# Conditioning columns turned by VectorE in PSUM, router weights asked for later, GpSimd's product in three parts, and early loads for the second and fourth expert

## What is computed

```
mod = silu(c) @ w_ada + b_ada            # 6 x 1024 columns
shift_m, scale_m, gate_m, shift_f, scale_f, gate_f = split(mod, 6)
h = rms_norm(x, g_mix) * (1 + scale_m) + shift_m
x = x + gate_m * hybrid_mixer(h)         # h @ w_in; sparse + forgetting attention; @ w_out
h = rms_norm(x, g_ffn) * (1 + scale_f) + shift_f
x = x + gate_f * hierarchical_moe(h)     # 4 groups x 8 experts, 2 experts for a token
```

## Time and profile before

| | |
|---|---|
| timed, median of 3 runs | 787.77 us (786.98 to 788.53) |
| profiled execution, its own time | 783.2 us |
| its span (first to last instruction) | 781.3 us |
| TensorE busy | 746.2 us, 96% of the span, 3945 matmul records |
| VectorE busy | 351.7 us, 45% |
| ScalarE busy | 190.3 us, 24% |
| GpSimd busy | 56.2 us, 7% |
| DMA, over the whole span | 197.25 MB, mean 252 GB/s |

### The profile page before, as it was taken

How to read it: one execution, slowest core, us unless ns; L and a number is a source line. 1 busy time by engine, 2 the same in 40 slices (tenths; PEclk the granted TensorE clock), 3 DMA queues, 4 the chain that set the end, 5 groups by cost and what they waited for, 6 DMA issues and landing times.

```text
span 781.3 us, 9778 instructions
## 1 busy us (share of the span) xinstructions
PE 746.2 (96%) x3945; PEld 493.8 (63%) x3945; DVE 351.7 (45%) x751; ACT 190.3 (24%) x419; POOL 56.2 (7%) x56
## 2 busy tenths in 40 slices
PE   5999999999899999999979999999999999999996
PEld 3687778877433334343434688688888888885442
DVE  2026475664631212121211595455166565657445
ACT  5113332452411101110111408313141111111002
POOL 2213644000000000000001000000000000000000
PEclk9899999999999999999999999999999999999999
DMA  9896994644949999999999990233254636352401
GB/s 346 273 362 243 352 353 172 254 162 171 416 169 419 412 418 415 416 417 415 417 413 385 370 352 13 99 108 108 89 190 153 192 131 215 120 205 107 162 27 57
DMA packets 76632, 197.25 MB, mean 252 GB/s; under 512 B 3263, under 2 KB 37416, under 8 KB 70184
## 3 DMA queue, kind: packets, MB, share of 16 engines
q1 hardware_dynamic: 75632, 195.37, 66.4%
q0 software_dynamic: 288, 0.41, 0.4%
q10 hardware_dynamic: 664, 0.80, 0.4%
HBM read 195.33 MB, written 1.05 MB: 251 GB/s over the span
## 4 chain that ended last, share of the span: by engine, by line
PE 81%; SPq 8%; DMA 4%; DVE 4%; ACT 2%; issue 1%; DVEq 0%; ACTq 0%
PE ps L1495 17%; PE ps L1215 10%; PE ps L759 9%; PE ps L1556 8%; PE ps L901 8%; PE ps L1289 5%; SPq L575 4%; PE ps L1129 4%; DMA arena<-in_w_up 2%; SPq L581 2%; DMA ring<-in_w_in 2%; PE ps L779 2%; PE ps L912 2%; PE ps L1298 2%; PE ps L1091 2%; PE ps L1101 2%
## 5 line engine op out<-in xcount | busy, mean ns | idle before, releaser
L1215 PE MATMUL ps<-ring,arena 128*64 128x512 f32 x352 | 77.6, 593 | 2.1 <-DMA ring<-in_w_up 2.1
L901 PE MATMUL ps<-hs,ring 128*128 128x256 f32 (+1 forms) x288 | 69.5, 397 | 2.9 <-DMA ring<-in_w_in 2.9
L901 PEld LDWEIGHTS ps<-hs,ring 128*128 128x128 f32 (+1 forms) x288 | 54.0, 192 | 15.7 <-issue 9.4
L1215 PEld LDWEIGHTS ps<-ring,arena 128*64 128x64 f32 x352 | 25.9, 137 | 52.2 <-issue 52.2
L2826 DVE SCALAR_TENSOR_TENSOR arena<-arena,own_rows,ps 128x256 f32<-128x256 f32 x16 | 7.7, 481 | 111.2 <-ACT arena L1889 111.2
L759 PE MATMUL ps<-hs,ring 128*128 128x256 f32 x240 | 53.3, 381 | 0.3 <-PE ps L759 0.3
L759 PEld LDWEIGHTS ps<-hs,ring 128*128 128x128 f32 x240 | 45.2, 190 | 7.1 <-issue 0.9
L1495 PE MATMUL ps<-ring,hs 128*128 128x256 f32 x176 | 41.7, 380 | 0.9 <-DVE xT L2701 0.9
L1495 PE MATMUL ps<-ring,mixT 128*128 128x256 f32 x176 | 41.7, 380 | 0.0
L1495 PE MATMUL ps<-arena,mixT 128*128 128x256 f32 x176 | 41.6, 379 | 0.0
L1289 PE MATMUL ps<-ring,arena 128*64 128x512 f32 x176 | 40.2, 598 | 1.0 <-issue 0.5
(11 more groups left out here) (492 smaller groups left out, 1236.3 us busy)
## 6 DMA issues: line engine op xcount, KB each, us to landing
ring<-in_w_down SPq DMA_DIRECT2D x23, 1024.0 KB, 19.3
ring<-in_w_gate_up SPq DMA_DIRECT2D x22, 1024.0 KB, 7.4
ring<-in_w_gate SPq DMA_DIRECT2D x20, 1024.0 KB, 16.6
ring<-in_w_up SPq DMA_DIRECT2D x20, 1024.0 KB, 17.6
ring<-in_w_ada SPq DMA_DIRECT2D x5, 3072.0 KB, 14.3
ring<-in_w_down SPq DMA_DIRECT2D x5, 2048.0 KB, 7.9
ring<-in_w_in SPq DMA_DIRECT2D x9, 1024.0 KB, 18.5
ring<-in_w_ada SPq DMA_DIRECT2D x16, 512.0 KB, 11.0
```

What stands on the lines that cost most here:

```text
L901: last = pe.matmul(o[0:n, 0:L], lhsT=w[:, k, lo:lo + n], rhs=h[:, k, :], start=k == 0, stop=k == KT - 1)
L1215: last = pe.matmul(ps[WIN * h:WIN * (h + 1), 0, :].rearrange("p (g n) -> p g n", g=2), lhsT=xw[:, u, k, :], rhs=expert_gate_up(2 * n + h, ...
```

## The change

Five things change.

1. **Turning.** `quarters` now reads its moving operand as blocks of 32 columns with 96 left out between them, so that each group of 32 partitions holds the features of the quarters of every tile that belong to it. A 32x32 transpose on VectorE then turns rows into columns: for `scale_m` and `shift_m` from PSUM into SBUF (`row0`, 128x256), for the chunks in place in PSUM bank 7 (128x192). `ada_select`, `ada_cols` and ScalarE's copies are gone. What `ada_cols` did for the router behind chunks 3 and 4 stays, as `shift_f_products`.
2. **The start.** In the place of `ada_select(0)` stand four products 128x512 whose result nobody reads, as soon as the tokens are turned. The first load of chunk 0 is split in two (200 columns, then 128), and the order of the three features follows.
3. **Router weights.** The five loads and the memset ahead of them move behind GpSimd's work on chunk 0. Its work on each chunk becomes three products of 128x768 by a column and two sums, in the place of one product of 128x2304 and two sums.
4. **Early loads.** SP loads parts of experts 1 and 3 (the second and the fourth) earlier, two of them behind the last loads of the attention and two while the output products run.
5. **Experts.** `clear_banks` is no longer called: the first product into each bank half starts the sum instead. In odd teams one of the eight tiles of `combine_joined` moves ahead of the activation's turn.

The diff, cut to its core (`step`, `Q` = 32, `P` = 128, `L` = 256, `KT` = 8):

```diff
             load_ada0("scale", ADA_HALF)
-            sp.dma_start(w[:, :, 0:328], in_d[:, :, IQ + 256:BQ]).then_inc(in0_first, 16)
+            sp.dma_start(w[:, :, P:328], in_d[:, :, IQ + 384:BQ]).then_inc(in0_first, 16)
+            sp.dma_start(w[:, :, 0:P], in_d[:, :, IQ + 256:IQ + 384]).then_inc(in0_second, 16)
             load_ada0("shift", 0)
...
+            load_down(1)
+            load_down(3)
             sp.wait_ge(ada_rows_done, 9)
             load_gate_up(0)
...
+            sp.wait_ge(ob_done, 2)
+            load_half(1, 1)
+            sp.wait_ge(ob_done, 4)
+            load_half(3, 1)
             sp.wait_ge(mo_done, 4)
-            load_gate_up(1)
-            load_down(1)
+            load_half(1, 0)
...
             sp.wait_ge(mo_done, KT)
-            load_gate_up(3)
-            load_down(3)
+            load_half(3, 0)
...
-            pool.wait_ge(tile_ready, 1)
-            pool.memset(wr[:, :, GROUPS:GROUP_COLS], 0.0).then_inc(pad_ready, 1)
-            pool.dma_start(wr[:, :, 0:GROUPS], w_group[0].rearrange("(k p) g -> p k g", p=P)).then_inc(wr_there, 16)
...
-                pool.tensor_tensor(w[:, PE_K:KT, :], w[:, PE_K:KT, :],
-                                   silu_c[:, PE_K:KT].unsqueeze(2).broadcast_to([P, n, ada_width(c_)]), ALU.mult
-                                   ).then_inc(pool_step, 1)
+                pool.tensor_scalar(w[:, PE_K, :], w[:, PE_K, :], silu_c[:, PE_K:PE_K + 1], None, ALU.mult).then_inc(pool_step, 1)
+                pool.wait_ge(pool_step, step.up())
+                pool.tensor_scalar(w[:, PE_K + 1, :], w[:, PE_K + 1, :], silu_c[:, PE_K + 1:PE_K + 2], None, ALU.mult).then_inc(pool_step, 1)
                 pool.wait_ge(pool_step, step.up())
                 pool.tensor_tensor(w[:, PE_K, :], w[:, PE_K, :], w[:, PE_K + 1, :], ALU.add).then_inc(pool_step, 1)
-                pool.wait_ge(pool_step, step.up())
+                pool.tensor_scalar(w[:, PE_K + 2, :], w[:, PE_K + 2, :], silu_c[:, PE_K + 2:PE_K + 3], None, ALU.mult).then_inc(pool_step, 1)
+                pool.wait_ge(pool_step, step.up(2))
                 pool.tensor_tensor(w[:, PE_K, :], w[:, PE_K, :], w[:, PE_K + 2, :], ALU.add).then_inc(ada_pool_ready, 1)
+                if c_ != 0:
+                    continue
+                pool.memset(wr[:, :, GROUPS:GROUP_COLS], 0.0).then_inc(pad_ready, 1)
+                pool.dma_start(wr[:, :, 0:GROUPS], w_group[0].rearrange("(k p) g -> p k g", p=P)).then_inc(wr_there, 16)
...
             def quarters(bank, lhsT, rhs, first=False, last=False):
 
+                parts = rhs.rearrange("p (m g i) -> p m g i", g=4, i=Q)
                 n = rhs.shape[1] // 4
                 for g in range(4):
-                    mm = pe.matmul(ps[Q * g:Q * g + Q, bank, 0:n], lhsT=lhsT, rhs=rhs[:, n * g:n * g + n], start=first,
-                                   stop=last, skip_group_check=True)
+                    mm = pe.matmul(ps[Q * g:Q * g + Q, bank, 0:n].rearrange("p (m i) -> p m i", i=Q), lhsT=lhsT,
+                                   rhs=parts[:, :, g, :], start=first, stop=last, skip_group_check=True)
...
-            def ada_select(bank):
-
-                pe.wait_ge(row_taken, bank + 1)
-                for i in range(2):
-                    last = pe.matmul(ps[:, bank, i:KT:2], lhsT=row0[:, bank, i * P:(i + 1) * P], rhs=all_rows,
-                                     start=True, stop=True)
...
-            ada_select(0)
+            pe.wait_ge(xT_ready, 2)
+            for _ in range(4):
+                pe.matmul(ps[:, 3, :], lhsT=ones[:], rhs=xn[:, 1, 512:D], start=True, stop=True)
...
             features(0, 256, 72, h=h0, first=True)
+            features(0, P, h=h0)
+            pe.wait_ge(in0_second, 16)
             features(0, 0, h=h0)
-            features(0, P, h=h0)
             shift_tiles()
             chunk_there("in", 0)
-            features(0, chunk_q, h=h0, amid=lambda: ada_select(1))
+            features(0, chunk_q, h=h0)
...
             ada_rows(1)
             features(2, P)
-            ada_cols(1)
             turn_probs(0)
...
             ada_rows(3)
             features(3, P)
-            ada_cols(3)
+            shift_f_products(3)
             turn_probs(2)
...
                     last = pe.matmul(ps[:, 4 + t // 2, (t % 2) * L:(t % 2 + 1) * L], lhsT=y[:, (t % 4) * P:(t % 4 + 1) * P],
-                                     rhs=p, start=False, stop=False, skip_group_check=True)
+                                     rhs=p, start=m == 0 and t % 2 == 0, stop=False, skip_group_check=True)
...
                 if u:
                     turn_puts(m)
+                    if n > 1:
+                        combine_joined(m - 1, JOINED[5:6])
...
                 if n > 1:
-                    combine_joined(m - 1, JOINED[5:8] if u else JOINED[3:5])
+                    combine_joined(m - 1, JOINED[6:8] if u else JOINED[3:5])
...
                 gate_up(0, 0, first=True).then_inc(gu_done, 1)
-                clear_banks()
                 pe.wait_ge(act_ready, 2)
...
-            def take_row(c):
-                act.wait_ge(ada_rows_done, c + 4)
-                act.activation(row[:, 0:ada_width(c) // 4], ps[:, 7, 0:ada_width(c) // 4], ACT.Copy).then_inc(row_taken, 1)
...
-            ve.wait_ge(ada_done, 1)
-            ve.tensor_tensor(mod[:, 8:16], ps[:, 0, 0:KT], parA[:, b_lo + 8:b_lo + 16], ALU.add).then_inc(dve_step, 1)
+            ve.wait_ge(ada_rows_done, 1)
+            ve.transpose(row0, ps[:, 0, 0:KT * Q]).then_inc(dve_step, 1)
+            own()
+            ve.tensor_tensor(mod[:, 8:16], row0[:, 0:KT * Q:Q], parA[:, b_lo + 8:b_lo + 16], ALU.add).then_inc(dve_step, 1)
...
             def add_bias(c):
 
-                at, m = ada_columns(c)
-                ve.wait_ge(ada_done, c + 4)
+                n, m = ada_width(c) // 4, ADA_AT[c] // P
+                m = slice(m, m + n // Q)
+                ve.wait_ge(ada_rows_done, c + 4)
+                ve.transpose(ps[:, 7, 0:n], ps[:, 7, 0:n]).then_inc(row_taken, 1)
+                ve.wait_ge(row_taken, c + 3)
...
```

More of the change, by code:

```diff
@@ L293, in build @@
         xn = mixT[:].rearrange("p k t -> p (k t)").rearrange("p (b d) -> p b d", b=BLK)
-        row0 = cut(5888, 2, 256)
+        row0 = cut(5888, KT * Q)
         h0 = hs[:, 1]
@@ L298, in build @@
         fix = cut(6480, 5)
-        row = tokf[:, 1536:1728]
-        even_rows, odd_rows, all_rows = ident[:, 0:P:2 * Q], ident[:, Q:P:2 * Q], ident[:, 0:P:Q]
+        all_rows = ident[:, 0:P:Q]
         out_tmp = cut(8192, 2, 2, L)
@@ L733, in _ @@
+                pool.wait_ge(pool_step, step.up(2))
                 pool.tensor_tensor(w[:, PE_K, :], w[:, PE_K, :], w[:, PE_K + 2, :], ALU.add).then_inc(ada_pool_ready, 1)
+                if c_ != 0:
+                    continue
+                pool.memset(wr[:, :, GROUPS:GROUP_COLS], 0.0).then_inc(pad_ready, 1)
+                pool.dma_start(wr[:, :, 0:GROUPS], w_group[0].rearrange("(k p) g -> p k g", p=P)).then_inc(wr_there, 16)
+                for g in range(GROUPS):
+                    pool.dma_start(wr[:, :, GROUP_COLS + PER_GROUP * g:GROUP_COLS + PER_GROUP * (g + 1)],
+                                   w_router[0, g].rearrange("(k p) e -> p k e", p=P)).then_inc(wr_there, 16)
@@ L858, in ada_rows, with shift_f_products @@
                 quarters(7, ones[:, 0:Q], w[:, PE_K, :], last=True).then_inc(ada_rows_done, 1)
-            def ada_cols(c):
-                at = ada_columns(c)[0]
-                pe.wait_ge(row_taken, c + 5)
-                if ada_width(c) == 6 * P:
-                    pe.matmul(ps[:, 7, at.start:at.stop:3], lhsT=row[:, 0:P], rhs=even_rows, start=True, stop=True)
-                    pe.matmul(ps[0:64, 7, at.start + 1:at.stop:3], lhsT=row[:, P:192], rhs=even_rows, start=True, stop=True)
-                    pe.matmul(ps[64:P, 7, at.start + 1:at.stop:3], lhsT=row[:, 0:64], rhs=odd_rows, start=True, stop=True)
-                    last = pe.matmul(ps[:, 7, at.start + 2:at.stop:3], lhsT=row[:, 64:192], rhs=odd_rows, start=True,
-                                     stop=True)
-                else:
-                    pe.matmul(ps[0:64, 7, at], lhsT=row[:, 0:64], rhs=even_rows, start=True, stop=True)
-                    last = pe.matmul(ps[64:P, 7, at], lhsT=row[:, 0:64], rhs=odd_rows, start=True, stop=True)
+            def shift_f_products(c):
+                pe.wait_ge(row_taken, c + 3)
                 if c == 3:
@@ L961, in _ @@
             tokens(1, 0, 260, (1,), amid=lambda: dots(1, 3))
-            ada_cols(0)
             chunk_there("in", 2)
@@ L1042, in _ @@
             features(3, 0)
-            ada_cols(2)
             turn_probs(1)
@@ L1059, in _ @@
             features(4, 0)
-            ada_cols(4)
+            shift_f_products(4)
             turn_probs(3)
@@ L1068, in _ @@
             features(4, P)
-            ada_cols(5)
             turn_probs(4)
@@ L1695, in _ @@
                                ACT.Copy).then_inc(xT_ready, 1)
```

(14 more changed lines are left out.)

50 lines of the change are left out of this document (20 added, 30 removed).

## The result

The changed kernel takes 779.57 us (median of four runs, 779.28 to 780.14), the kernel before in the same comparison 787.96 (786.98 to 788.53). The ratio is 0.9896 with a 95% interval of 0.9879 to 0.9913: 8.4 us or 1.0% faster.

A forecast was written before the change was run, and what follows sets the result against it. TensorE, busy 96% of the span, was taken as the bound, with weights in the expert stage. 0.5 + 2.9 + 0.35 + 2.8 + 0.45 = 7.0 us: profiled 783.2 becomes 776.2, plus 4.6 is 780.8 us; range 777.6 to 784.2.

The forecast's parts named there:

- The start: Before the shift rows: features start 0.5 us earlier, kept clock wins 2.9, dropped second turning 0.34 (0.35 in the sum).
- Chunk 0's rest: Rest of chunk 0's load: lands about 33.5 us, 1.4 to spare before TensorE asks at 34.9; costed at nothing.
- the rival: Chunk 0's rest still lands at 36.1, TensorE waits 1.2 us, gain 5.8, time 782.0 us; chance 12%.
- GpSimd's parts: GpSimd's three products and two sums per chunk: at most 1.4 us more, covered by 2.1 room at chunk 0; cost nothing.
- The router loads behind chunk 0: Router loads moved behind GpSimd's chunk 0 work: pass no other waiting load, wanted some 50 us later by chunk 3.
- The chunks' turning: Attention stages of chunks 1 to 5: small turning products gone, 4 x 0.64 + 0.21 = 2.8 us won.
- The experts: Expert stage: zeroing products hidden; moved tiles in odd teams given back to weights, only the last team's 0.45 us counts.
- the early loads: Earlier loads for the second and fourth expert: their products wait for nothing, nothing gained; bound half a microsecond.
- From the trace to the median: Whole kernel: timed median stands 4.6 us above the profiled execution, so 776.2 becomes 780.8 us.
- The slower rival: Quarter products, 18.4 us: 32-column reads slowed over 38% lose; at double time 11.4 us slower, 799.2; chance 6%.

## Why the prediction was right, and where it wasn't

The forecast was 780.8 us, the measurement 779.57, and the direction and the size agree. But that the number fits is luck. 7.0 us were summed up from terms of the trace, and between the traces there are 3.4. The rest came from a thing that the prediction didn't see: against the lower band of the kernel before, 782.6, the changed kernel wins 2.8 us.

- **The start, 0.5 + 2.9 + 0.35 us.** The size was right: 3.7 us up to the shift rows, 10.36 us for the features, clock at 1.00 from 18 to 27 us. The 2.9 us for the clock were 13.50 less 10.57, two times of 48 records in the trace of the kernel before; the changed kernel's 10.36 makes 3.1 of it. The reason was only half right. The split load does as much as the four products: without them the features end at the same 31.1 us, since a start at 18.90 makes up for a clock of 0.50 from 20 to 22 us. The first load had landed by then, not at the forecast 19.8.
- **Chunk 0's rest, at nothing.** Right: a wait of 0.27 us, though the load landed at 34.9 and not at 33.5. In the kernel before with the four products alone, the rival happened: 1.6 us.
- **GpSimd's parts, at nothing (bounds -0.3 to 1).** This step failed. I bounded a single-input product by a sum's 1.82 us; it takes 2.21, the work on a chunk 10.5 us. TensorE waits three times for it, 3.7 us in all: 0.76 at chunk 0, 1.73 at chunk 1 and 1.21 at chunk 2. I had looked for the least room at chunk 0 alone, and the longest wait is at chunk 1, whose load came late as well. And with the whole product back, the kernel is 1.6 us faster.
- **The router loads behind chunk 0, at nothing.** Also failed. I asked only which load waits behind them, and not whose bandwidth they take. There they fall into the loads for chunks 1 and 2. From TensorE's release of chunk 1's load to GpSimd's start on chunk 2 it is 28.6 us (62.25 to 90.83) against 25.3 before (65.06 to 90.34). The windows of TensorE (us, busy, granted clock, DMA share, GB/s), first of the changed kernel and then of the one before, catch it:

```profile
68.00:72.00 4.00, 2.47 (x19) 1.00 1.03 212
```

```profile
68.00:72.00 4.00, 3.25 (x24) 1.00 1.03 416
```

  The DMA engines are as busy (1.03) and move half as much (212 GB/s against 416). The two experiments with the whole product, 28.2 us with the router loads there and 25.3 with them moved away, put 2.9 us to them. With GpSimd's longer work this is where the start's 3.7 us went. In the timed runs the whole product is worth 1.6 us, and thirds of it with the router loads moved away 4.0.
- **The chunks' turning, 2.8 us.** Right: 2.2 us, from 101.90 to 142.69 against 101.85 to 144.86. Chunk 1's 0.64 was won too, and lost in the wait for GpSimd at chunk 2. VectorE's transposes took 0.45 us for the first two rows and 0.39 for a chunk, and nothing waited for them.
- **The experts, 0.45 us, and the early loads, 0.** Right in kind: the tiles are won team by team, 0.43 us each, and given back to the weights. Undoing either edit changes nothing that can be measured.
- **From the trace to the median.** Failed. The prediction took the 4.6 us between the profiled execution and the timed median as a constant. It wasn't one. It was the distance between two bands, made in the main by GpSimd's product and VectorE's scaling at chunk 2. The three parts take the upper band away, and so does the later load of chunk 2. The earlier trace rows had the contention, 2.64 us for 0.55, one chunk further on; I priced it there at 0.4 us at most (0.64 less 0.2) and did not ask what a product would do that starts 0.2 us earlier.

So the 8.4 us are 2.8 us in the lower band and 4.6 for the band itself, which the four runs of the kernel before in the first comparison all met; the last 1.0 is scatter of the few runs within the bands (787.96 against 787.2, 779.57 against 779.83). The slower rival, reading in pieces of 32 columns, didn't happen: a chunk's 48 records take 2.09 us as before.

## What to carry to other kernels

When the timed median and the profiled execution of a kernel differ by more than the runs do among themselves, look at the single runs before adding up terms: two bands can come from a race of two engines, of which one trace shows only one outcome (here medians of 782.6 and 787.2 us, and a scaling of 1.2 or 6.2 us). A small load moved out of one stage's way takes its DMA time somewhere else (here chunk 2 came after 28.2 us in the place of 25.3), so look for a stretch where the DMA engines are idle (here 56 to 62 us, a share of 0.02 in the changed kernel's trace), not for one where nothing waits behind it. And work cut into pieces so that it blocks less has to be priced as a new instruction: here the same product cost 4.03 us whole, 4.5 in thirds of the same kind, and 6.6 in single-input parts.

## What the runs showed of the hardware that was not expected

On GpSimd a product of 128x768 by a column as a single-input instruction took 2.21 us, slower than the same product with the column laid out as a second operand (1.47) and than a sum of two such tiles (1.81). A granted clock of 0.66 from 375 to 380 us came after a wait of 1.98 us in one execution; in another it stood at 1.00 there after a wait of 2.00 us at the same place (changed kernel run twice), so in these two the length of the wait alone doesn't tell whether it falls.
